# First stage of a decoder block on eight cores: x in two token halves, float32 weights of four z tiles in one queue with it

## What is computed

```python
h = rmsnorm(x, g_mix)
proj = einsum('bsd,de->bse', h, w_in)        # 3072 columns: u 1024, v 1024, z 1024
u, v, z = gelu(proj[..., :1024]), gelu(proj[..., 1024:2048]), proj[..., 2048:]
out_a = u * (tril(w_s) @ rmsnorm(v) + b_s)   # per head, in chunks of 128 positions
# out_b: trailing mean of z over 2, 4, 8 or 16 positions minus z, then w_pool and pool_scale
x = x + einsum('bse,ed->bsd', concat([out_a, out_b]), w_out)
h = rmsnorm(x, g_ffn)
x = x + square(relu(h @ w_up)) @ w_down      # hidden width 8192
return rmsnorm(x, g_final)
```

## Time and profile before

| | us |
|---|---|
| median of 3 runs | 1264.48 (1263.96 to 1264.93) |
| the profiled execution | 1264.68 |
| span of its slowest core, core 2 | 1263.1 |
| spans of all cores | 1257.0 to 1263.1 |
| PE busy (share of the span) | 1206.7 (96%) |
| DVE, ACT busy | 330.9, 249.0 |

### The profile page before, as it was taken

The page is one execution under the profiler, slowest core; times in us unless marked ns, Lnnn a source line. Parts: engine busy times, 40 slices in busy tenths (PEclk is TensorE's granted clock), DMA queues, the critical chain, the costliest instruction groups (busy, mean ns, idle before and its releaser), DMA issues.

```text
span 1263.1 us, 14288 instructions; the slowest of 8 cores (1257.0 to 1263.1 us)
## 1 busy us (share of the span) xinstructions
PE 1206.7 (96%) x5736; PEld 547.2 (43%) x5736; DVE 330.9 (26%) x550; ACT 249.0 (20%) x457; POOL 67.3 (5%) x100
## 2 busy tenths in 40 slices
PE   3899999899999999999999999999999999999993
PEld 0344444344444444444444444444444444444441
DVE  2636645411111212121121212112121211211234
ACT  3301187323221110001111000111100011123332
POOL 0100000100000000000000000000000000000000
PEclk9999999899999999999999999999999999999997
DMA  8995420886534433443453344345334434548775
GB/s 223 171 184 96 70 64 1 129 181 152 138 67 72 92 70 67 85 82 67 71 93 69 67 84 83 67 72 92 70 67 86 81 67 73 93 81 148 140 168 167
DMA packets 33745, 124.85 MB, mean 99 GB/s; under 512 B 2704, under 2 KB 2832, under 8 KB 33168
## 3 DMA queue, kind: packets, MB, share of 16 engines
q0 software_dynamic: 25472, 97.52, 44.5%
q1 hardware_dynamic: 8208, 26.41, 6.5%
HBM read 213.05 MB, written 8.39 MB: 175 GB/s over the span
## 4 chain that ended last, share of the span: by engine, by line
PE 92%; DMA 4%; ACT 1%; DVE 1%; issue 1%; SPq 0%; DVEq 0%; POOL 0%; ACTq 0%; POOLq 0%
PE ps L216 82%; PE ps L609 8%; DMA xf<-xT 2%; DMA ringall<-w_in 2%; PE ps L799 1%; DVE xr_h L765 0%; ACT L547 0%; DVE xr_mid L765 0%; PE ps L639 0%; PE ps L638 0%; ACT pooled L527 0%; DVE mtmp L500 0%; ACT sqv L557 0%; PE ps L345 0%; DVE vh L565 0%
## 5 line engine op out<-in xcount | busy, mean ns | idle before, releaser
L216 PE MATMUL ps<-h2T,ringall 128*128 128x512 bf16 x2048 | 442.8, 379 | 0.0
L216 PEld LDWEIGHTS ps<-h2T,ringall 128*128 128x128 bf16 x2048 | 200.4, 98 | 241.6
L216 PE MATMUL ps<-uT,ringall 128*128 128x512 bf16 x1024 | 234.1, 379 | 0.0
L216 PE MATMUL ps<-pooled,ringall 128*128 128x512 bf16 x1024 | 234.1, 379 | 0.0
L724 DVE SCALAR_TENSOR_TENSOR rtmp<-ps,rstd_bc 128x512 f32<-128x512 f32 x128 | 82.5, 686 | 360.8 <-PE ps L216 351.2
L216 PEld LDWEIGHTS ps<-pooled,ringall 128*128 128x128 bf16 x1024 | 100.2, 98 | 120.8
L216 PEld LDWEIGHTS ps<-uT,ringall 128*128 128x128 bf16 x1024 | 100.1, 98 | 120.7
L729 ACT ACTIVATE uT<-rtmp 128x512 bf16<-128x512 f32 x64 | 39.1, 630 | 505.9 <-DVE rtmp L724 505.9
L216 PE MATMUL ps<-hT,ringall 128*128 128x512 bf16 x512 | 116.2, 383 | 1.1 <-DMA ringall<-w_in 0.9
L216 PEld LDWEIGHTS ps<-hT,ringall 128*128 128x128 bf16 x512 | 49.7, 98 | 61.7 <-issue 4.4
L729 ACT ACTIVATE pooled<-rtmp 128x512 bf16<-128x512 f32 x64 | 39.3, 630 | 181.7 <-DVE rtmp L724 181.7
(11 more groups left out here) (102 smaller groups left out, 503.8 us busy)
## 6 DMA issues: line engine op xcount, KB each, us to landing
ringall<-w_down POOLq DMA_DIRECT2D x40, 1024.0 KB, 9.0
ringall<-w_up POOLq DMA_DIRECT2D x32, 1024.0 KB, 9.0
ringall<-w_in POOLq DMA_DIRECT2D x11, 1024.0 KB, 16.7
xf<-xT SPq DMA_DIRECT2D x4, 2048.0 KB, 19.9
ringall<-w_out POOLq DMA_DIRECT2D x8, 1024.0 KB, 14.8
xstage<-xT SPq DMA_DIRECT2D x16, 512.0 KB, 10.1
outT<-xr_h SPq DMA_DIRECT2D x16, 256.0 KB, 4.0
outT<-xr_mid SPq DMA_DIRECT2D x16, 256.0 KB, 5.3
```

What stands on the lines that cost most here:

```text
L216: ins = e.matmul(ps[:, banks[sel], c0:c1], lhsT, rhs, start=st, stop=sp_)
```

## The change

The host lays x out in two token halves, and the kernel holds it so. SP's queue, which waits for nothing, alternates four pieces of weights (tiles 0 to 3 of z, four chunks each, float32, 1 MB) with four pieces of the first half of x (1 MB); then the halo's x and constants, then four pieces of the second half. DVE casts the weights into slots 0 and 1 of the ring. POOL's load of tiles 4 and 5 waits for the second piece of the second half, those of the next slabs for the fourth.

Each half goes through its 16 chunks; for each chunk PE runs one stat matmul and one matmul of each of the four tiles, into four banks. The four evictions of the first half are put before (tiles 0, 1) and into (tiles 2, 3) the work of the second half. The halo's scalings become one instruction; the halos of tiles 0 to 3 are computed after tile 4, the columns of rstd after tile 6. Pooling of chunk m - 4 follows tile m. The second load of x takes two rows of 512 tokens in place of one of 1024.

```diff
-    slab0a = [P.dma("pool", lambda e: e.dma_start(out=ringall[:, 0, :, :], in_=w_in_d[:, 16, :, :]), "slot0a")]
-    x_ld = []
-    for q in range(4):
-        x_ld.append(P.dma("sp", lambda e, q=q: e.dma_start(out=xf[:, 4 * q:4 * q + 4, :], in_=xT_d[:, 4 * q:4 * q + 4, :]),
-                          "x%d" % q, [slab0a[0]]))
+    def load_x(half, q):
+        x_ld[half].append(P.dma("sp", lambda e: e.dma_start(
+            out=xf[:, half, KG * q:KG * q + KG, :], in_=xT_d[:, half, KG * q:KG * q + KG, :]), "x%d%d" % (half, q)))
+
+    for q in range(KC // KG):
+        wf_ld.append(P.dma("sp", lambda e, q=q: e.dma_start(
+            out=wstg[:, q, :, :].rearrange("p n (k c) -> p n k c", c=128), in_=w_in_d[:, 16:20, KG * q:KG * q + KG, :]), "wf%d" % q))
+        load_x(0, q)
...
+    for q in range(KC // KG):
+        load_x(1, q)
...
-    nxt = [0]
+    nxt = [2]
...
-                deps.append(x_ld[3])
...
+                deps.append(x_ld[1][1 if n == 2 else 3])
...
+    for half in range(2):
+        st = None
         for k in range(KC):
+            q = k // KG
+            if half == 0 and k % KG == 0:
+                wz_cast[q] = P.add("dve", lambda e, q=q: e.tensor_copy(
+                    out=ringall[:, 0:4, KG * q:KG * q + KG, :].rearrange("p n k c -> p n (k c)"), in_=wstg[:, q, :, :]), [wf_ld[q]])
+                slab_ld[0] = slab_ld[1] = wz_cast[q]
+            st = h_chunk(half, k)
+            d = [wz_cast[q], h_ops[half][k]]
+            if k == 0:
+                d += [bank_last[b] for b in z_banks[half]]
+
+            def z_fn(e, half=half, k=k):
+                ins = None
+                for m in range(4):
+                    ins = e.matmul(ps[:, z_banks[half][m], :], ringall[:, m, k, :], hT[:, k, half * 512:(half + 1) * 512],
+                                   start=(k == 0), stop=(k == KC - 1))
+                return ins
+            z_job[half] = P.add("pe", z_fn, d)
+            if half == 1 and k == 1:
+                z_evac_half(2, 0, z_job[0], z_banks[0][2])
+                z_evac_half(3, 0, z_job[0], z_banks[0][3])
+            if half == 1 and k == 3:
+                sqh_op = P.add("dve", lambda e: e.tensor_tensor(out=sqh[:, :, :], in0=xh[:, :, :], in1=xh[:, :, :], op=ALU.mult), [cst1])
...
+        r1[half] = rstd_chain(st, half)
+        if half == 0:
+            z_evac_half(0, 0, z_job[0], z_banks[0][0])
+            z_evac_half(1, 0, z_job[0], z_banks[0][1])
...
+    for m in range(4):
+        z_evac_half(m, 1, z_job[1], z_banks[1][m])
...
+    halo_after = {4: [0, 1, 2, 3], 5: [4, 5], 7: [6, 7]}
...
+    for m in range(4, 8):
...
+        if m in halo_after:
+            ms = halo_after[m]
+            hj = z_halo_job(ms)
+            z_evac_halo(ms, hj)
+            for i in ms:
+                slab_done[i // 2] = hj
+            issue_loads(ms[-1] // 2 + NSLOT)
+        if m == 6:
+            rc_evac = rstd_columns()
+        pooling_chunk(m - 4)
```

More of the change, by code:

```diff
@@ L269, in issue_loads @@
             else:
-                deps.append(x_ld[3])
[L271 to L275, removed]
+                deps.append(x_ld[1][1 if n == 2 else 3])
+            slab_ld[n] = P.dma("pool", lambda e, n=n: e.dma_start(out=ringall[:, 2 * (n % NSLOT):2 * (n % NSLOT) + 2, :, :], in_=slabs[n]),
+                               "slot%d" % (n % NSLOT), deps)
             nxt[0] += 1
@@ L300, in stat_chunk @@
         else:
[L301 to L312, removed]
@@ L325, in build_program, with rstd_chain @@
-    h_ops = [None] * KC
-    n1_mm = [None]
-    z_evac = [None] * 8
+            sq = P.add("dve", lambda e: e.tensor_tensor(out=sq_slot(s), in0=src_ap, in1=src_ap, op=ALU.mult), list(src_deps) + [sq_reader[s]])
+        d = [sq, ones_op]
+        if k == 0:
+            d.append(bank_last[6 + half])
+        pe = P.add("pe", lambda e: e.matmul(ps[:, 6 + half, :], ones[:, :], sq_slot(s), start=(k == 0), stop=(k == KC - 1)), d)
+        sq_reader[s] = pe
+        return pe
+    def rstd_chain(pe_op, half):
+        c0, c1 = half * 512, (half + 1) * 512
+        s1 = P.add("act", lambda e: e.activation(out=rstd_bc[:, c0:c1], in_=ps[:, 6 + half, :], func=AF.Ln, bias=EPSB, scale=1.0 / D),
+                   [pe_op, eps_op])
+        bank_last[6 + half] = s1
+        return P.add("act", lambda e: e.activation(out=rstd_bc[:, c0:c1], in_=rstd_bc[:, c0:c1], func=AF.Exp, scale=-0.5), [s1])
@@ L328, in build_program @@
+    h_ops = [[None] * KC, [None] * KC]
+    z_evac = [[] for _ in range(8)]
     zh_last = [None]
     last_rstd_reader = [None]
[L331 to L339, removed]
@@ L341, in z_halo_job, with z_evac_half, z_evac_halo @@
-    def z_halo_job(m, n, mmi):
+    r1 = [None, None]
+    def z_evac_half(m, half, job, bank):
+        c0, c1 = half * 512, (half + 1) * 512
+        ev = P.add("dve", lambda e: e.tensor_tensor(out=zE[:, m, HALO + c0:HALO + c1], in0=ps[:, bank, :], in1=rstd_bc[:, c0:c1], op=ALU.mult), [job, r1[half]])
+        bank_last[bank] = ev
+        z_evac[m].append(ev)
+        last_rstd_reader[0] = ev
+    def z_evac_halo(ms, hjob):
+        lo, n = ms[0], len(ms)
+        ev = P.add("dve", lambda e: e.tensor_tensor(
+            out=zE[:, lo:lo + n, 0:HALO], in0=ps[:, 7, lo * HALO:(lo + n) * HALO].rearrange("p (m t) -> p m t", m=n),
+            in1=rstd_h[:, :].unsqueeze(1).broadcast_to([128, n, HALO]), op=ALU.mult), [hjob, hs2])
+        bank_last[7] = ev
+        for m in ms:
+            z_evac[m].append(ev)
@@ L342, in halo_fn, with z_halo_job, halo_rstd, halo_stat @@
+    def z_halo_job(ms):
         def halo_fn(e):
             ins = None
+            for m in ms:
+                for k in range(KC):
+                    ins = e.matmul(ps[:, 7, m * HALO:(m + 1) * HALO], RS(m // 2, k, (m % 2) * 128, (m % 2 + 1) * 128), hh[:, k, :],
+                                   start=(k == 0), stop=(k == KC - 1))
+            return ins
+        return P.add("pe", halo_fn, [slab_ld[m // 2] for m in ms] + [hh_all, bank_last[7]])
+    sqh_op = hh_all = hs2 = None
+    def halo_rstd():
+        def halo_stat(e):
+            ins = None
@@ L344, in halo_fn @@
             for k in range(KC):
-                ins = e.matmul(ps[:, 7, m * HALO:(m + 1) * HALO], RS(n, k, mmi * 128, (mmi + 1) * 128), hh[:, k, :],
-                               start=(k == 0), stop=(k == KC - 1))
-            return ins
[L348 to L363, removed]
@@ L377, in build_program @@
[L377 to L386, removed]
+                ins = e.matmul(ps[:, 6, 0:HALO], ones[:, :], sqh[:, k, :], start=(k == 0), stop=(k == KC - 1))
@@ new lines, in halo_stat @@
+            return ins
+        hs_pe = P.add("pe", halo_stat, [sqh_op, ones_op, bank_last[6]])
+        hs1 = P.add("act", lambda e: e.activation(out=rstd_h[:, :], in_=ps[:, 6, 0:HALO], func=AF.Ln, bias=EPSB, scale=1.0 / D), [hs_pe, eps_op])
+        bank_last[6] = hs1
+        hs2 = P.add("act", lambda e: e.activation(out=rstd_h[:, :], in_=rstd_h[:, :], func=AF.Exp, scale=-0.5), [hs1])
+        return hs2
+    z_banks = [[take_bank() for _ in range(4)] for _ in range(2)]
+    z_job = [None, None]
@@ new lines, in h_chunk @@
+    def h_chunk(half, k):
+        xk = xf[:, half, k, :]
+        hk = hT[:, k, half * 512:(half + 1) * 512]
+        ld = x_ld[half][k // KG]
+        if k % 2 == 0:
+            h_ops[half][k] = P.add("act", lambda e: e.activation(out=hk, in_=xk, func=AF.Copy, scale=vecs[:, G_MIX + k:G_MIX + k + 1]), [ld, vecs_ld])
+            return stat_chunk(k, half, xk, [ld], "dve")
+        h_ops[half][k] = P.add("dve", lambda e: e.tensor_scalar(out=hk, in0=xk, scalar1=vecs[:, G_MIX + k:G_MIX + k + 1], scalar2=None, op0=ALU.mult), [ld, vecs_ld])
+        return stat_chunk(k, half, xk, [ld], "act")
@@ L412, in pooling_chunk, with rstd_columns, col_fn @@
         pool_ops[c] = f2
-    c1 = P.add("dve", lambda e: e.tensor_copy(out=rs_hi[:, :], in_=rstd_bc[0:1, :]), [r1[0]])
+    def rstd_columns():
+        bc = take_bank()
+        def col_fn(e):
+            ins = None
+            first = True
+            for i in range(8):
+                for t in (rs_hi, rs_lo, rs_lo2):
+                    ins = e.matmul(ps[:, bc, i:i + 1], t[0:1, i * 128:(i + 1) * 128], ones[0:1, 0:1], start=first, stop=(i == 7 and t is rs_lo2))
+                    first = False
+            return ins
+        col_pe = P.add("pe", col_fn, [c1, c3, c5, ones_op, bank_last[bc]])
+        ev = P.add("act", lambda e: e.activation(out=rstd_col[:, :], in_=ps[:, bc, 0:8], func=AF.Copy), [col_pe])
+        bank_last[bc] = ev
+        return ev
+    for m in range(4):
+        z_evac_half(m, 1, z_job[1], z_banks[1][m])
+    c1 = P.add("dve", lambda e: e.tensor_copy(out=rs_hi[:, :], in_=rstd_bc[0:1, :]), [r1[1]])
     c2 = P.add("dve", lambda e: e.tensor_tensor(out=rsr[:, :], in0=rstd_bc[0:1, :], in1=rs_hi[:, :], op=ALU.subtract), [c1])
@@ L418, in build_program @@
     c5 = P.add("dve", lambda e: e.tensor_copy(out=rs_lo2[:, :], in_=rsr[:, :]), [c4])
```

(26 more changed lines are left out.)

55 lines of the change are left out of this document (24 added, 31 removed).

## The result

The median fell from 1264.53 us to 1257.29 us (four runs each), a ratio of 0.9946 with a 95% interval of 0.9931 to 0.9961: 7.2 us, where 8.0 were forecast. The profiled execution took 1256.82 us; the span of its slowest core, core 3, is 1255.3 us against 1263.1.

The account below looks back on a forecast made before the run. DMA was taken to bound the kernel up to 53.9 us and PE after that. With u starting 8.0 us earlier, 1264.7 - 8.0 = 1256.7, and 0.2 lower for the median: 1256.5 us, range 1251.5 to 1262.5.

Parts of the forecast that it names:

- Where the time is: Whole kernel: DMA sets the time to 53.9 us, PE after; first u tile at 90.7 us in place of 98.65.
- The eighth piece at 30.9 us: SP's queue at the start: the last piece of x's first half lands at 1.44 + 29.4 = 30.9 us.
- rival B: Loads at the start: float32 weights in short rows take 7.0 us per MB, 14.0 us later, 1270.5 us; chance 0.06.
- Casts, squares, scalings hidden: First half, each group of four chunks: DVE needs 3.4 to 4.5 us of 7.0, ACT 2.8, so hidden.
- Last group: First half's last four chunks: from 31.7 us, 4.3 us of PE work plus 1.0 for the clock, to 37.0 us.
- The turn: Between the halves: PE idle 2.9 us, to 39.9 us, for rstd, two evictions and a square; bounds 2.5 and 4.
- Half 1: Second half's 16 chunks: PE bound, 17.3 us plus 1.3 for the clock and 0.3 for x, to 58.8 us.
- The other four tiles: After the first four tiles: 31.9 us with moved halos and rstd columns, so u starts at 90.7 us.
- The queue share: x's last piece beside POOL's slab: x gets a fifth, lands at 52 us; rival: 3 us late, 1259.5 us, chance 0.12.
- Rival A (clock): Chunked work never holds the full clock: last group +3.3 us, second half +3, 1263 us; chance 0.10.

Follow-up runs that it names:

- Weights by POOL: Changed kernel with the weights of tiles 0 to 3 as casting loads in POOL's queue, x alone in SP's: mean span 1267.4 us, 14.7 above the changed kernel.
- the early start: Kernel before, with SP's loads of x no longer waiting for the first weight tile: mean span 1256.7 us, 2.6 below the kernel before.
- the four tiles: Changed kernel with SP's first piece waiting for an unused 1 MB weight load by POOL: mean span 1259.5 us, 0.2 below the kernel before.

## Why the prediction was right, step by step

- *Where the time is*: right. The first u tile moved by 6.9 us on the slowest cores (90.7 forecast, 91.73 measured). The stages behind took 1155.9 us from its first eviction before and 1156.1 after, the mean of eight cores.
- *How close the number is*: in part luck. On the slowest cores u came 1.0 us later than forecast, and the stages behind took 0.9 us less (1157.4 us from u's first eviction on core 2 before, 1156.5 on core 3 after), which I had not forecast: 7.8 us in the spans for 8.0. The mean of the eight cores moved less, u's first eviction from 104.27 to 97.91 us and the span from 1260.2 to 1254.1. The cores lay further apart before (1257.0 to 1263.1 us, after it 1252.3 to 1255.3), and I had worked from the slowest.
- *The eighth piece at 30.9 us*: it landed at 32.28. The slow part was the beginning: DVE's cast of the first weights began at 9.28 us and x's first square at 13.11, where 3.5 us a piece gave some 5.5 and 9, so that PE began at 13.94 us and not near 11; behind that the pieces came every 3.3 us. Weights in rows of 2 KB took no longer than x: DVE took up the later weight pieces 2.7 to 3.1 us behind the x piece ahead of them, x 3.3 to 3.7 behind the weights (rival B is out).
- *Casts, squares, scalings hidden*: right, and sizes were right to some 0.1 us:

```profile
L312 DVE TENSOR_TENSOR sqr<-xf x16: 682/691/693, 13.1 to 53.5; 128x512 bf16<-128x512 f32 x16
L385 DVE TENSOR_SCALAR hT<-xf,vecs x16: 478/480/544, 13.7 to 54.2; 128x512 bf16<-128x512 f32 x16
```

  The cast of 2048 elements took 1.23 us (ns min/median/max in the rows above; it was 1.36 or 2.45).
- *Last group*: 33.27 to 37.75 us, 4.3 of work at full clock on core 3, so that the 1.0 for the clock was not due there and made up for part of the late landing; on cores 2 and 6 it was more. *The turn*: 2.83 for 2.9. *Half 1*: from 40.58 to 59.53, 18.95 for 18.9, of which 1.6 is the clock (I had taken 1.3 for it and 0.3 for a wait for x that did not come; my 52.8 us for when x's last piece is wanted leaves out the 1.3 that it says are in it). *The other four tiles*: 32.0 for 31.9. From the eighth piece to u it was 59.5 us for 59.8.
- *The queue share*: wrong, without a cost. I had taken SP's part beside a slab as a fifth, from xstage's landings, and x's last piece at 52 us. It landed by 47.5, when POOL's next load went out. The slab went out at 41.13 us, not 38.4, and hardly moved before 44: from 43 to 44 us it had 4 packets beside x's 35. By then x was nearly through, so the share was not put to the test here. Weights by POOL shows it: packet by packet, and x's rows are 8 KB where xstage's were 4.
- *Rival A (clock)*: true of one place on each of six cores, not of the stretch. In the changed kernel's profile 6 of 18 waits of 1.6 to 2.8 us ahead of a group were followed by a fall, and each fall to 1.2 GHz lasted one stretch of 3 to 4 us. So a loss of 1.6 us, not of 6. All cores also began at 1.2 GHz and ran so until 17 to 21 us, which cost nothing, as each had to wait for the last piece of x's first half anyway. The Trainium skill (TensorE: Matmul & The Clock Gate, HAM oscillation) speaks of bursts shorter than the DMA wait behind them; the groups of 4.3 us here were longer than any wait between them, so its case was not this one, and my prediction should not have held the rule against the chunked work.
- What I did not see: that the two parts of the change hang on each other. The forecast was the sum of both, so it did not need it. Alone the early start gives 2.6 us by the mean span and the four tiles 0.2.

## What to carry to other kernels

In this stage, where loads pace PE, two numbers counted: when the piece lands behind which no wait is left, and how much work stands behind it. An earlier first piece was worth nothing alone, and neither was work put under the loads that brought its own bytes ahead of them. Where a stage's two halves share accumulators, look for the turn: give the second half its free banks first, and put its first inputs ahead of the evictions in each engine's queue; here that gave 3.2 us more, half of what the whole change gave. Put loads that must arrive in a certain order into one queue: split over two they cost 14.7 us here.

## What the runs showed of the hardware

Two DMA queues shared the engines packet by packet, not byte by byte: 145 packets (1.06 MB, mostly rows of 8 KB) beside 144 (0.15 MB, rows of 1 KB as landed) from 14 to 18 us. The clock's fall behind the same wait of 2.83 us came on some cores and not on others of the same execution, on 4 of 8 in both profiles of the changed kernel. And the first two pieces of SP's queue, 2 MB, took 11.6 us from the first issue, where the following pairs took 6.2 to 6.8.
